# Decoder step with a 128x128 expert layer: respacing the gather steps of the second phase

## The reference, cut to what matters

```
q = (hb @ w_peer_q).reshape(PEER_BLOCK, PEER_HEADS, 2, PEER_HALF)
...
idx = (e1 * N_KEYS + e2).reshape(PEER_BLOCK, PEER_HEADS * PEER_TOPK)
g = jax.nn.softmax(top_s, axis=-1).reshape(PEER_BLOCK, PEER_HEADS * PEER_TOPK)
u_rows = jnp.take(expert_u, idx, axis=0)
a = jnp.einsum('td,tkd->tk', hb, u_rows, preferred_element_type=F32)
wgt = (g * jax.nn.gelu(a, approximate=False)).astype(hb.dtype)
v_rows = jnp.take(expert_v, idx, axis=0)
return jnp.einsum('tk,tkd->td', wgt, v_rows)
```

## Time and profile before

| | |
|---|---|
| median of 3 runs | 2310.26 us (2307.82 to 2310.28) |
| the profiled execution | 2310.29 us, of which the span 2308.5 us |
| PE busy | 1636.2 us (71%) |
| DVE busy | 1469.3 us (64%) |
| ACT busy | 905.0 us (39%) |
| POOL busy | 757.7 us (33%) |
| DMA | 756.65 MB, of which 570.46 MB on the queue of the gathers |
| mean granted clock of PE | 0.801 of full speed |

### The profile page before, as it was taken

How to read it: one execution, slowest core, us unless ns; L and a number is a source line. 1 busy time by engine, 2 the same in 40 slices (tenths; PEclk the granted TensorE clock), 3 DMA queues, 4 the chain that set the end, 5 groups by cost and what they waited for, 6 DMA issues and landing times.

```text
span 2308.5 us, 32870 instructions
## 1 busy us (share of the span) xinstructions
PE 1636.2 (71%) x11544; PEld 742.5 (32%) x11544; DVE 1469.3 (64%) x3591; ACT 905.0 (39%) x2426; POOL 757.7 (33%) x713
## 2 busy tenths in 40 slices
PE   7999999996898978777778988883433433343343
PEld 3556655443343434434333433330000000000000
DVE  2587663124558687878887767346767765766764
ACT  2132233012455445554657543333433433333332
POOL 1354100001333343333433333333443443344342
PEclk9999999998899988888988999895555555555555
DMA  5333555657898989899999999999999999999998
GB/s 193 121 121 123 183 193 221 238 189 257 302 406 326 376 310 374 310 369 372 351 378 358 377 392 408 398 419 371 391 399 396 390 401 367 405 381 403 400 387 356
DMA packets 130336, 756.65 MB, mean 328 GB/s; under 512 B 16852, under 2 KB 43084, under 8 KB 50412
## 3 DMA queue, kind: packets, MB, share of 16 engines
q0 software_dynamic: 78336, 570.46, 62.7%
q1 hardware_dynamic: 51836, 184.09, 21.5%
HBM read 734.70 MB, written 20.64 MB: 327 GB/s over the span
## 4 chain that ended last, share of the span: by engine, by line
PE 33%; DMA 26%; DVE 25%; issue 8%; ACT 5%; POOL 1%; SPq 0%; DVEq 0%; ACTq 0%; POOLq 0%
DMA ring<-in_expert_uv,pick 24%; PE z L1151 19%; DVE ring L1875 6%; PE acc L1305 4%; PE z L1157 2%; DMA sx<-in_x_prompt 1%; PE o L1186 1%; PE o L1239 1%; DVE cand L1817 1%; DVE e L1818 1%; DVE cand L1815 1%; ACT wgt L1471 1%; DVE ti L1780 1%; PE s L1203 1%; DVE ti L1783 1%
## 5 line engine op out<-in xcount | busy, mean ns | idle before, releaser
L1083 POOL DMA_INDIRECT ring<-in_expert_uv,pick x544 | 623.6, 1146 | 986.0 <-PE acc L1305 908.3
L1875 DVE CUSTOM_DVE_ANT_0 ring<-ring,rep 128x1024 f32<-128x1024 f32 x544 | 660.5, 1225 | 382.5 <-DMA ring<-in_expert_uv,pick 352.7
L1305 PE MATMUL acc<-ring,fold 128*32 128x256 f32 x4352 | 462.8, 516 | 507.6 <-ACT fold L1473 505.7
L1151 PE MATMUL z<-wts,hT 128*128 128x384 f32 (+1 forms) x1408 | 616.4, 575 | 8.1 <-ACT hT L1482 5.3
L1469 ACT ACTIVATE gel<-dots 128x1 f32<-128x1 f32 x544 | 110.3, 203 | 763.7 <-DVE dots L1875 760.2
L1305 PEld LDWEIGHTS acc<-ring,fold 128*32 128x32 f32 x4352 | 105.2, 125 | 831.6 <-ACT fold L1473 764.8
L1151 PEld LDWEIGHTS z<-wts,hT 128*128 128x128 f32 x1408 | 261.1, 199 | 261.1 <-issue 197.5
L1151 PE MATMUL z<-wts,yT 128*128 128x512 f32 x384 | 192.9, 638 | 14.9 <-ACT yT L1663 7.5
L1473 ACT ACTIVATE fold<-cst,wgt 128x32 f32<-128x32 f32 x544 | 175.7, 323 | 17.6
L1471 ACT ACTIVATE wgt<-gel,pick 128x1 f32<-128x1 f32 x544 | 161.3, 296 | 17.8
L1772 DVE SCALAR_TENSOR_TENSOR yT<-uT,vec,yT 128x256 f32<-128x256 f32 x240 | 107.8, 502 | 2.3
(11 more groups left out here) (230 smaller groups left out, 1743.4 us busy)
## 6 DMA issues: line engine op xcount, KB each, us to landing
wts<-in_w_qkv SPq DMA_DIRECT2D x24, 1536.0 KB, 7.7
wts<-in_w_glu SPq DMA_DIRECT2D x8, 2048.0 KB, 9.7
wts<-in_w_gate SPq DMA_DIRECT2D x8, 2048.0 KB, 11.8
wts<-in_w_wq SPq DMA_DIRECT2D x8, 2048.0 KB, 11.4
ring<-in_k_cache SPq DMA_DIRECT2D x8, 1536.0 KB, 9.8
ring<-in_v_cache SPq DMA_DIRECT2D x8, 1536.0 KB, 8.1
rep<-x_h SPq DMA_DIRECT2D x68, 128.0 KB, 10.0
ring<-in_expert_uv,pick POOLq DMA_INDIRECT x544, 11.3
```

Of the source, the lines that this page charges most:

```text
L1083: eng.indirect_dma_start(ring[:, i % RING, :], None, a["expert_uv"], bass.IndirectOffsetOnAxis(picks(i, 0).bitcast(U32), 0)).then_inc(row_ ...
L1151: mm = eng.matmul(bank[:, 0:w], of[:, k, :], rows[:, k, :], start=(k == 0), stop=(k == depth - 1))
L1305: mm = eng.matmul(acc[b][SUB * c:SUB * (c + 1), col:col + 256], fold[:, i % 4, :], ring[:, i % RING, D + 256 * c:D + 256 * (c + 1)], start ...
L1875: eng.tensor_tensor_reduce(u, u, rep[:, j, :], 1.0, 0.0, ALU.mult, ALU.add, dots[:, i % 4:i % 4 + 1]).then_inc(dot_ready, 1)
```

## The change

The share of a tick is no longer proportional to its PE work alone. `loads_by_tick` is new: it spreads, over the ticks of each unit, an estimate (`LOAD_US`) of the time that the next unit's weights take to stream. A step is put at `ROW_US` = 2.66. The sum of both over the phase is divided in proportion to PE work, each tick's load is taken off its part, and what is left (at least a tenth of its PE work) is its share of the steps. The marks still run from 16 to 272, and nothing else is changed in the code.

```diff
+LOAD_US = {"glu": 5.3, "qkv": 4.0, "gate": 5.3, "cp": 5.3, "ap": 2.7, "wo": 5.3, "wq": 5.3}
+ROW_US = 2.66
+
+
+def loads_by_tick():
+
+    out = np.zeros(len(TICKS))
+    for n, tick in enumerate(TICKS):
+        for v in tick:
+            if v[0] == "mm":
+                of = unit_of(v[1])
+                if of + 1 < len(UNITS):
+                    after = UNITS[of + 1]
+                    out[n] += LOAD_US[after[0]] * (v[3] - v[2]) / (MM[v[1][0]] * len(PAIRS[after[1]]))
+    return out
...
     lo, hi = marks[ENDS[0] - 1], BASE[2] - LAG
-    rest = np.cumsum(cost[ENDS[0]:])
+    work, loads = cost[ENDS[0]:], loads_by_tick()[ENDS[0]:]
+    both = loads.sum() + ROW_US * (hi - lo)
+    rest = np.cumsum(np.maximum(work * both / work.sum() - loads, 0.1 * work))
     for n in range(ENDS[0], len(TICKS)):
         marks[n] = lo + int((hi - lo) * rest[n - ENDS[0]] / rest[-1] + 1e-9)
```

## The result

The changed kernel takes 2337.5 us (median of 4 runs, 2333.71 to 2345.42) against 2310.27 us before: ratio 1.0115, 95% interval 1.0098 to 1.0133. It is 27 us slower; forecast were 2308.3 us and a range up to 2319. The profiled execution took 2345.42 us, 8 us above that median, so its differences come out somewhat larger: the spans of the two profiles differ by 35.1 us. Lines of the code have numbers 19 higher than before (L1305 is now L1324).

What follows compares the result with a forecast made beforehand. Gathers were taken to set the pace from ap to wq and in the tail, PE in cp, and chained waits earlier; +4.6, -0.6, -10.0 and +4.0 make -2.0 us, giving 2308.3 us from 2310.29, range 2299 to 2319 us.

Steps and rivals of the forecast that it cites:

- glu and qkv: Early stretch, 641.8 to 1193.8 us: 4 steps more at 1.14 us each, +4.6 us (2.3 to 10.8).
- at no cost of its own: Claim that norm tasks, searches, softmax, picks and score and token loads moving with the steps add 0 us.
- in the chain's price as far as it counts: Claim that shifted top-16 parts on DVE and softmax on ACT are already covered by the price per step.
- keep their distance to the steps that need them: Claim that pick tasks, moved one to five ticks earlier, follow the marks and so cost nothing extra.
- First gate units: First three gate units: 32 steps before and after, so no change in time.
- last gate unit with cp: Last gate unit and cp: 1 step fewer at PE's 0.57 us, -0.6 us (to -2.7).
- ap to the third wq unit: Stretch after cp, gathers setting the pace: 5 steps fewer at 2.0 us each, -10.0 us (-2.9 to -13.6).
- The last wq unit and what follows: From the last wq unit on: 2 steps more at 2.0 us each, +4.0 us (1.1 to 5.4).
- Faster rival: Late stretch pays in full, early steps hide: 2301.7 us, some 2 us less per restart spared; chance 0.32.
- No change: Every step costs PE's 0.57 us wherever it stands, net 0 steps: 2310.3 us; chance 0.12.
- Slower rival: Steps added behind heavy ticks cost 2.71 us of landing each: +8.6 us, 2318.9 us; chance 0.20.
- The signs: Observations named beforehand as showing the forecast right or wrong, such as qkv 3 to 5 us longer at DMA share above 0.92.

Runs made afterwards that it cites:

- e13: Changed kernel's marks, but searches, softmax numerators, score loads and spreads at the old ticks, so only gather steps move: 2326.69 us (1.0058).
- e8: Kernel before with old marks to the end of qkv, four extra steps over the first three gate units, then the changed kernel's marks: 2310.62 us.
- e7: Kernel before, same steps per stretch, but inside each stretch steps shifted from heavy to light ticks: 2318.79 us (1.003).
- e14: Kernel before with its old marks, but searches, softmax numerators, score loads and spreads at the changed kernel's ticks; no step moved: 2335.94 us (1.0106).
- e15: e8's marks, but searches, softmax numerators, score loads and spreads kept at the old marks' ticks: 2317.46 us (1.0021).

## Why the prediction was wrong

- **glu and qkv, +4.6 us (2.3 to 10.8): measured +37.1 us. This is the step that failed**, in two places. I priced a moved step at 1.14 us, between PE's 0.57 and the landing's 2.71, as if a step cost its own time and no more, and I put what moves along with the steps "at no cost of its own". The runs show two prices in its place. The searches with their spreads cost 25.7 us when they move without the steps; I had put the searches "in the chain's price as far as it counts". And the steps without them cost 16.4 us, 19.0 us in qkv for three more there, over 6 us each. My upper bound of 2.71 us counted the late row and nothing queued behind it. Half rows take about half of the 19.0 us away; how the rest comes about is not shown. DVE's own waits for rows in qkv grew by 4.6 us only (21.2 to 25.8 us in e13).
- **The picks "keep their distance to the steps that need them"**: true and beside the point. They also keep their two ticks to the last part of the search, but DVE was not through with it when PE came to the spread: the waits for the spread rose from 13.6 to 23.1 us, and later spreads win back 10 to 17 us of the whole.
- **First gate units, 0: -2.9; last gate unit with cp, -0.6: +1.5.** Together -1.4 us. The time ahead of the first moved tick, where nothing differs, came out 2.5 us longer (641.8 to 644.3 us), so amounts of this size are not told from nothing.
- **ap to the third wq unit, -10.0 us (-2.9 to -13.6): -7.8** (5.7 + 2.1). Right in size, and in part by its own reason: the hT wait at the start of wo is gone, but DVE's row waits fell by 1.7 us only, and of the 5.7 us in ap with wo 4.5 are PE's busy time (62.99 to 58.52 us, four steps fewer at a clock of 0.97 for 0.94).
- **The last wq unit and what follows, +4.0 us: +4.7**, 0.1 in the unit and the rest behind it (from there to the end of the span 748.5 us before, 753.1 after). The number came, but not in its place: I had expected the unit longer and the part after the last tick unchanged. With the 2.5 us ahead, 37.1 - 1.4 - 7.8 + 4.7 make the 35.1 us between the spans.
- **Faster rival** (early steps hide): fell. **No change** (PE's 0.57 us everywhere): fell; even in gate and cp e8's four steps more, less one in cp, took 5.6 us. **Slower rival** (heavy ticks become the wait): right in sign, and in a part of its mechanism, since half rows take half of the steps' own loss away. That the heavy ticks make it was not borne out by e7, which thinned them and lost. Its price, 2.71 us a step and +8.6 us in all, was a third of the loss, and it did not see the search and the spread.
- **The signs** that I named: qkv was to be 3 to 5 us longer at a DMA share above 0.92. It was 32 us longer at 0.88, and "an early stretch longer by 8 us or more with fold waits well over 35.6 us" is the case that came.

The Trainium skill's bound of about 358 GB/s (DMA: Bandwidth & Descriptors, section Bandwidth), by which the early stretch was full, would also have given a slower kernel. The trace does not bear it out as the reason: qkv moved 338 GB/s when it lost, less than the 352 before, and later stretches again 406 and 418.

What stays open: why the steps' own loss does not go away wholly with half rows (9 us of 19 stay), how the loss of e14 is shared between the search and the spread, and which of the 42 parts cost most. No placing that beats the kernel before was found.

## What to carry to other kernels

Before you move one kind of work along a hand-written order, list all that is indexed by it: here the searches, softmax numerators and spreads moved with the step numbers, and moving them without the steps cost about as much as the whole change (25.7 us, the whole 27). Price a moved task on an engine that works in order by what stands behind it there and who waits for that, not by its own duration. A lower DMA share together with more idle time on PE and DVE was the mark of such mutual waiting here. A pair of runs that moves the carrier (the steps) and the riders (what hangs on them) apart is the way to tell which it is, with one run for each rider.

## What the runs showed of the hardware

PE's pauses also cost clock. In the four ticks from 339 on the granted clock was full before and 0.79 after:
```profile
947.50:962.70 15.20, 12.50 (x90) 7.54 (x90) 12.38 (x39) 8.95 (x27) 8.96 (x7) 1.00 0.87 338
```
```profile
953.20:977.40 24.20, 16.64 (x98) 9.18 (x98) 20.41 (x61) 13.51 (x32) 9.19 (x8) 0.79 0.95 352
```
Four records of a tick, 1.56 us before (958.74 us), took 2.62 us behind a stop of 2.13 us and 2.78 us behind one of 4.92 us (PE in order of time, after):
```profile
960.99 1.08 PE L1324 MATMUL acc<-ring,fold 128*32 128x256 f32 x8 [2.13 <-ACT fold L1492]
962.00 2.62 PE L1170 MATMUL z<-wts,hT 128*128 128x384 f32 x4
...
969.87 1.12 PE L1378 MATMUL t<-cst,sx 128*128 128x128 f32 x4 [4.92 <-ACT kvr L1501]
970.92 1.08 PE L1324 MATMUL acc<-ring,fold 128*32 128x256 f32 x8
971.93 2.78 PE L1170 MATMUL z<-wts,hT 128*128 128x384 f32 x4
```
That is near the lower of its two levels, 1.2 of 2.4 GHz. Over qkv the granted clock fell from 0.88 to 0.84, and PE's work took 8.1 us longer than the three steps explain (9.8 - 1.7). In e14, with no step moved, it took 8.8 us longer at 0.85, in e13 13.1 us of the 19.0, also at 0.85. How much of this lengthens the stretch is not shown: e8 and e15, the same program up to there, both take 408.0 us, with PE busy for 312.8 us at 0.88 and for 318.6 us at 0.85.
